# Gate products of a recurrent block: fp32 matmuls, or three products of high and low halves split on GpSimd

## What is computed

```
gate_br, x_br = split(h @ w_in, 2)                      # w_in: 1024 x 2560
gate_br = gelu(gate_br)
xc = conv_b + sum(xp[:, j:j+S] * conv_w[j] for j in range(4))      # causal, 1280 channels
r = sigmoid(einsum('bsnd,nde->bsne', xc, ga_w) + ga_b)  # 10 blocks of 128 x 128
i = sigmoid(einsum('bsnd,nde->bsne', xc, gx_w) + gx_b)  # 10 blocks of 128 x 128
log_a = -8 * r * softplus(-lam)
a, mult = exp(log_a), sqrt(-expm1(2 * log_a))
h_t = a_t * h_(t-1) + mult_t * (i * xc)_t               # scan over the tokens
out = (h * gate_br) @ w_out
```

## Time and profile before

| | |
|---|---|
| time, median of 3 runs | 1376.95 us (1376.85 to 1377.02) |
| profiled execution, its own time | 1376.97 us |
| its span in the profile | 1375.1 us |
| TensorE busy | 1361.9 us (99%) |
| VectorE busy | 1119.8 us (81%) |
| ScalarE busy | 930.9 us (68%) |
| GpSimd busy | 89.2 us (6%) |
| DMA | 319 GB/s in the mean |
| granted TensorE clock | 0.998 |
| recurrent block, projections and gates | 315 to 376 us of the span |

### The profile page before, as it was taken

The page is one execution under the profiler, slowest core; times in us unless marked ns, Lnnn a source line. Parts: engine busy times, 40 slices in busy tenths (PEclk is TensorE's granted clock), DMA queues, the critical chain, the costliest instruction groups (busy, mean ns, idle before and its releaser), DMA issues.

```text
span 1375.1 us, 18249 instructions
## 1 busy us (share of the span) xinstructions
PE 1361.9 (99%) x6778; PEld 1152.6 (84%) x6778; DVE 1119.8 (81%) x952; ACT 930.9 (68%) x734; POOL 89.2 (6%) x89
## 2 busy tenths in 40 slices
PE   9999999999999999999999999999999999999997
PEld 9988888889988888888888888888888888888885
DVE  6776554458979999898888989889898898989896
ACT  5756444445858777777777777777777677777764
POOL 4000000001220000000000000000000000001130
PEclk9999999999999999999999999999999999999999
DMA  9535655652569999999999999999999999999993
GB/s 309 188 132 174 214 186 189 236 178 93 184 236 368 411 401 366 395 407 345 391 393 361 370 394 411 336 398 390 360 377 386 411 340 397 389 356 381 409 367 120
DMA packets 147266, 438.33 MB, mean 319 GB/s; under 512 B 7267, under 2 KB 30428, under 8 KB 147218
## 3 DMA queue, kind: packets, MB, share of 16 engines
q1 hardware_dynamic: 142848, 423.39, 81.6%
q0 software_dynamic: 4304, 14.27, 3.4%
q10 hardware_dynamic: 66, 0.02, 0.0%
HBM read 429.35 MB, written 8.40 MB: 318 GB/s over the span
## 4 chain that ended last, share of the span: by engine, by line
PE 97%; DMA 1%; ACT 1%; DVE 1%; issue 0%; POOLq 0%; SPq 0%; DVEq 0%; ACTq 0%
PE ps L1936 29%; PE ps L1525 27%; PE ps L1941 14%; PE ps L1953 14%; PE ps L1958 7%; PE ps L1977 2%; DMA work<-in_moe_w_down_dram 1%; PE ps L1816 1%; PE ps L2037 0%; PE ps L1611 0%; PE ps L1741 0%; DMA xres<-in_x_dram 0%; PE ps L1874 0%; ACT w_hi L532 0%; PE ps L1581 0%
## 5 line engine op out<-in xcount | busy, mean ns | idle before, releaser
L532 ACT ACTIVATE w_hi<-w_ring 128x2048 fp32r<-128x2048 f32 (+1 forms) x258 | 487.6, 1902 | 162.2 <-PE ps L1941 90.3
L1395 DVE TENSOR_TENSOR w_lo<-w_ring,w_hi 128x2048 fp32r<-128x2048 f32 x190 | 433.7, 2301 | 56.2 <-ACT w_hi L532 55.8
L532 ACT ACTIVATE w_hi<-work 128x2048 fp32r<-128x2048 f32 x144 | 275.3, 1918 | 122.7 <-PE ps L1958 63.7
L1395 DVE TENSOR_TENSOR w_lo<-work,w_hi 128x2048 fp32r<-128x2048 f32 x141 | 322.7, 2302 | 39.7 <-ACT w_hi L532 39.2
L1936 PE MATMUL ps<-w_hi,xt_hi 128*128 128x512 f32 x896 | 289.5, 393 | 0.8 <-ACT xt_hi L532 0.8
L1936 PE MATMUL ps<-w_hi,xt_lo 128*128 128x512 f32 x896 | 286.8, 390 | 0.0
L1941 PE MATMUL ps<-w_lo,xt_hi 128*128 128x512 f32 x896 | 239.7, 389 | 0.0
L1953 PE MATMUL ps<-w_hi,split 128*128 128x512 f32 x864 | 214.4, 390 | 0.2 <-DVE split L1405 0.2
L1936 PEld LDWEIGHTS ps<-w_hi,xt_lo 128*128 128x128 f32 x896 | 168.2, 188 | 35.4
L1941 PEld LDWEIGHTS ps<-w_lo,xt_hi 128*128 128x128 f32 x896 | 168.2, 188 | 35.3
L1936 PEld LDWEIGHTS ps<-w_hi,xt_hi 128*128 128x128 f32 x896 | 165.8, 188 | 33.9 <-issue 1.0
(11 more groups left out here) (293 smaller groups left out, 1177.6 us busy)
## 6 DMA issues: line engine op xcount, KB each, us to landing
w_ring<-in_moe_w_up_dram SPq DMA_DIRECT2D x72, 1024.0 KB, 8.8
w_ring<-in_moe_w_down_dram SPq DMA_DIRECT2D x72, 1024.0 KB, 6.8
work<-in_moe_w_gate_dram SPq DMA_DIRECT2D x64, 1024.0 KB, 8.2
w_ring<-in_moe_w_gate_dram SPq DMA_DIRECT2D x48, 1024.0 KB, 7.9
work<-in_moe_w_up_dram SPq DMA_DIRECT2D x40, 1024.0 KB, 8.7
work<-in_moe_w_down_dram SPq DMA_DIRECT2D x40, 1024.0 KB, 6.7
w_ring<-in_attn_w_qkv_dram SPq DMA_DIRECT2D x11, 1024.0 KB, 11.2
w_ring<-in_ffn_w_gate_dram SPq DMA_DIRECT2D x11, 1024.0 KB, 5.1
```

What stands on the lines that cost most here:

```text
L532: return nc.scalar.activation(out, in_, ACT.Copy)
L1395: V.tensor_tensor(w_lo[:, half_slot(n), :], land(n), w_hi[:, half_slot(n), :].bitcast(F32), ALU.subtract).then_inc(lo_ready, 1)
```

## The change

The gates take the form of the other products. The gate weights and the convolved inputs are split into a high half (fp32r) and the rest, both on GpSimd. The halves lie in parts of `split` that are free at that time; `wga_lo` takes columns of `aT_hi` and so waits for `piece_used`, `P_IN`. `split_xc(j)` has one buffer and waits for the gates of the pair before (`ri_ps`). PE waits for `wg_lo` instead of `in_lru` ahead of the second piece, and for `xc_lo_ok` instead of `xc_ok` ahead of the gates.

```diff
+        wga_lo = split[:, 0:1280].rearrange("p (n e) -> p n e", n=RB)
+        xc_hi = split[:, 1280:1792].rearrange("p (n t) -> p n t", n=2)
+        xc_lo = split[:, 1792:2304].rearrange("p (n t) -> p n t", n=2)
+        wga_hi = split[:, 2304:3584].rearrange("p (n e) -> p n e", n=RB)
+        wgx_hi = split[:, 3584:4864].rearrange("p (n e) -> p n e", n=RB)
+        wgx_lo = split[:, 4864:6144].rearrange("p (n e) -> p n e", n=RB)
...
+            pool.wait_ge(in_lru, 32)
+            for hi, w in ((wga_hi, wga), (wgx_hi, wgx)):
+                nc.gpsimd.tensor_copy(hi, w).then_inc(wg_hi, 1)
+            pool.wait_ge(wg_hi, 2)
+            nc.gpsimd.tensor_tensor(wgx_lo, wgx, wgx_hi.bitcast(F32), ALU.subtract).then_inc(wg_lo, 1)
+            pool.wait_ge(piece_used, P_IN)
+            nc.gpsimd.tensor_tensor(wga_lo, wga, wga_hi.bitcast(F32), ALU.subtract).then_inc(wg_lo, 1)
+
+            def split_xc(j):
+                pool.wait_ge(xc_ok, j + 1)
+                if j:
+                    pool.wait_ge(ri_ps, j)
+                nc.gpsimd.tensor_copy(xc_hi, xc[:, j % 2]).then_inc(xc_hi_ok, 1)
+                pool.wait_ge(xc_hi_ok, j + 1)
+                nc.gpsimd.tensor_tensor(xc_lo, xc[:, j % 2], xc_hi.bitcast(F32), ALU.subtract).then_inc(xc_lo_ok, 1)
+
             for j in range(RB // 2):
+                split_xc(j)
                 pool.wait_ge(ri_ok, 2 * j + 2)
...
-            pe.wait_ge(in_lru, 32)
+            pe.wait_ge(wg_lo, 2)
 
             def gates(j):
-                pe.wait_ge(xc_ok, j + 1)
+                pe.wait_ge(xc_lo_ok, j + 1)
                 if j:
                     pe.wait_ge(t_ok, 2 * j)
                 for m in range(2):
-                    for w, bank in ((wga, 2), (wgx, 3)):
-                        ins = T.matmul(ps[:, bank, 256 * m:256 * m + 256], w[:, 2 * j + m, :], xc[:, j % 2, m, :],
-                                       start=True, stop=True)
+                    b = 2 * j + m
+                    for wh, wl, bank in ((wga_hi, wga_lo, 2), (wgx_hi, wgx_lo, 3)):
+                        ins = mm3(ps[:, bank, 256 * m:256 * m + 256], xc_hi[:, m, :], xc_lo[:, m, :], wh[:, b, :], wl[:, b, :],
+                                  True, True, True)
```

More of the change, by code:

```diff
@@ L351, in build_trunk @@
         sroot_ps, sroot_ok = sem("sroot_ps"), sem("sroot_ok")
+        wg_hi, wg_lo, xc_hi_ok, xc_lo_ok = sem("wg_hi"), sem("wg_lo"), sem("xc_hi_ok"), sem("xc_lo_ok")
         root_ps, gate_raw, ixs_ok = sem("root_ps"), sem("gate_raw"), sem("ixs_ok")
```

## The result

The changed kernel took **1390.01 us** (median of 6, 1388.80 to 1391.32) against 1376.95: ratio 1.0095, 95% interval [1.0085, 1.0105]. That is 13 us slower; 1381.9 was forecast, with 1388.5 as the upper end. The direction was right, the size was not. The six times lie in two groups, three at 1388.8 and three at 1391.2 to 1391.3. The profiled execution is of the second: 1391.22 us, span 1389.4, clock 0.993.

What follows compares the result with a forecast made beforehand. TensorE was taken to bound the kernel, with VectorE close behind. Gate stalls of 2.75 + 1.0 + 0.8 + 1.0 + 0.8 = 6.35 us, less 1.45 gained, added 4.9 to 1376.97: 1381.9 us, range 1376.5 to 1388.5.

Steps and rivals of the forecast that it cites:

- Twelve products: TensorE's gates: 1.44 us a pair instead of 1.73 for four fp32 products, 1.45 us gained over five pairs.
- The conversion: GpSimd's high half of xc: taken as 0.6 us, with bounds of 0.6 and 2.4 us.
- the subtraction: GpSimd's low half of xc: priced at 1.15 to 1.2 us of work by the same engine's tensor_tensor.
- The weights' split: GpSimd's split of the gate weights: ends by 312.8, PE asks at 315, so it costs nothing.
- its race against w_lo in pair 0: First gates: w_lo runs until 322.48, then the subtraction; PE starts at 323.8 instead of 321.05, a 2.75 us stall.
- The conversion hides beside w_lo in this sum if it isn't excluded too: Pair 0's split on GpSimd: the 0.6 us conversion runs during VectorE's w_lo and adds nothing to the 2.75 us stall.
- I go by the row: Choice against B: a w_lo starting inside a one-input GpSimd tensor_scalar took its usual 2.28 us; own forecast 45%.
- rival B: Conversion of xc excluded beside w_lo too: stalls sum to 10.5 us, less 1.45, giving 1386.0 us; chance 28%.
- odd pairs: Gates of pairs 1 and 3: the split arrives behind ix, stalling PE 1.0 us each; B had 0.7.
- the range's margin: The only place where a clock fall after TensorE's waits was counted; range 1376.5 to 1388.5 us.
- no row shows it fall after a wait of 3 us: TensorE's clock: taken as full over this stretch; a fall would come on top of B or C.
- C: Conversion of xc costs its upper bound, 2.4 us: stalls sum to 15.0 us, less 1.45, giving 1390.5 us; chance 10%.

Runs made afterwards that it cites:

- spread3: spread2 with the first half of the third piece's w_lo moved behind the next four xt_lo; 1375.55 us, ratio 0.9990.
- spread2: Changed kernel with the pairs' work moved from GpSimd to ScalarE and VectorE, w_lo halved, third w_lo and table load earlier, first gates inside next piece; 1376.63 us.
- act_cast: Changed kernel with the conversion of xc on ScalarE instead of GpSimd, the subtraction staying on GpSimd; 1381.68 us.
- warm: Changed kernel with dummy products on TensorE into an unused PSUM bank ahead of each gate wait; 1386.20 us.
- again: Changed kernel executed once more for its profile, with only a blank line added in the source; 1388.83 us.
- split_first: Changed kernel, but VectorE starts the w_lo behind each xc only when GpSimd has split that xc; 1387.21 us.
- pool_alone: Changed kernel with all of GpSimd's new work, but TensorE keeping its four fp32 gate products and waiting for xc as before; 1380.12 us.
- after: The changed kernel itself, in its profiled execution, of the slower group of times; 1391.22 us.
- idle: Kernel before, fp32 gates and nothing split, with TensorE held ahead of gates 0, 2 and 4 by GpSimd memsets of unused columns; 1387.10 us.
- pe_alone: Changed kernel with twelve products a pair but no split of xc on GpSimd, its low part left out; weights still split; 1376.41 us.

## Why the prediction was wrong, point by point

**Right.** Twelve products cost 1.44 us, and 5 x 0.29 is the gain wherever TensorE sets the round (spread3). The conversion costs 0.60 us, by the copies of the earlier trace rows; the subtraction 1.26. The weights' split is free: it ended at 311.5, and PE didn't wait at 315 (spread2 shows what it costs when a w_lo half stands beside it). That the subtraction loses its race against w_lo in pair 0: act_cast, which leaves just that, had its first gates at 323.68 for my 323.8. act_cast's time of 1381.7 does not prove the rest of the sum, since its later pairs went by another chain.

**The step that failed** is "The conversion hides beside w_lo in this sum if it isn't excluded too", and the choice behind it, "I go by the row". It is excluded. The first stall was 3.22 us for my 2.75 and rival B's 3.45, the second 2.16 for my 0.8 and B's 1.75, and the last 4.1 for my 0.8 and B's 3.9, since the conversion came between the first and the second of the three w_lo, the subtraction between the second and the third. The waits were 9.5 us for my 6.35. warm's time is B's sum to 0.2 us, but in part by balance: against rounds of 7.19 us its five gates came 3.3, 1.2, 1.4, 1.2 and 3.4 us later, where B had 3.45, 0.7, 1.75, 0.7 and 3.9. B was wrong on the odd pairs, in which `ix` went ahead of w_lo. The Trainium skill, page "SBUF — State Buffer", section "Who interferes with whom", has a VectorE instruction with two SBUF inputs contend with a GpSimd instruction that reads SBUF; the runs agree (2.61 against 0.60 us, and 0.61 in all five pairs once w_lo stood behind). I had set against it one row, a GpSimd tensor_scalar beside an undisturbed w_lo. What I had not looked at is that row's beginning. In the trace of before, the w_lo ahead of it:

```profile
1303.68 3.90 DVE L1395 TENSOR_TENSOR w_lo<-work,w_hi 128x2048 fp32r<-128x2048 f32 x1 [1.85 <-ACT w_hi L532]
```

It had itself started beside a GpSimd tensor_tensor that ran from 1303.02 to 1305.43, and it ran until 1307.6, over the first 2.0 of the tensor_scalar's 4.78 us. The row so contains a stretch in which it may have been the one held, and may have been done with its reads when the next w_lo began at 1308.64. This was only argued, no run took it apart; but a row with such a neighbour could not carry the choice, and did not bound the conversion at 2.4 us either.

**The term that was missing** is the lower clock: 6.2 us of slow products in the profiled execution, 2.6 to 5.0 us in the time by warm, left in "the range's margin". The profiled execution lost 9.4 us more than my 4.9: 3.1 are the waits (9.5 for 6.35), 6.2 the clock. The sentence "no row shows it fall after a wait of 3 us" was true because the trace has no wait of 3 us, so it was no evidence. On top of B's 1386.0, 2.6 to 5.0 us give 1388.6 to 1391.0; that this is where both groups are is no second proof, since the cost was taken from these times. The range's upper end, 1388.5, was B with 2.5 us of margin: a cost that would come on top of B and could not be excluded should have been priced as one.

**A term that was mis-sized by luck**: odd pairs. I had 1.0 and B 0.7 for each; they had 0 in the profiled execution, and in again one of them 0.9. With TensorE at the lower level its round was stretched from 7.2 to 9.9 us, so that GpSimd had caught up: `ix`, conversion and subtraction of pair 1 were done at 332.95, and PE came at 334.2. Part of the price of the clock was paid with the stalls of the odd pairs (in warm, at full clock, they are back), so the two can't simply be added.

**A rival that came near by chance**: C, a conversion of 2.4 us everywhere, had 1390.5 us, and 1390.0 was measured. Its condition failed: with no w_lo in the way the conversion took 0.60 to 0.61 us (pairs 1 and 3 of the changed kernel, all five pairs of split_first).

**Overlooked**: VectorE has work with one SBUF tensor that GpSimd holds, the tensor_scalars. GpSimd's new work cost 3.2 us in pool_alone, where my sum had nothing for it. In the changed kernel it is hidden behind the stalls (VectorE stands for 4.56 and 3.60 us behind the two stretched rounds); it shows once these are gone.

## What to carry over

A chain of two short operations on GpSimd, handed over between VectorE instructions that read two SBUF tensors, costs the length of those instructions and not its own: 1.9 us of work arrived 4.0 us after `xc`. Before GpSimd is given work beside a VectorE that is busy for most of its round, price each of its instructions as if it started after the running VectorE one, and each following VectorE one as if it waited for it; then ask where TensorE will stand still, for behind the waits of 3.2 us here the lower clock took another 1.8 to 2.7. And a gain on the engine that bounds (0.29 of 7.48 us here) is only to be had when the next engine's round is shorter than the new one: here that took moving work between three engines, for 0.1%.

## What the hardware showed that I had not expected

- A VectorE tensor_scalar of 128x256 with one SBUF tensor was held by GpSimd: two took 1.64 to 1.66 us instead of 0.74 beside a subtraction (after, warm) and 2.65 beside a subtraction and `ix` (pool_alone). The six taps (two SBUF tensors each) took 3.6 to 3.8 instead of 2.7 beside `ix`. The Trainium skill, page "VectorE: DVE Perf Modes", section "Mode 2×_2P — use both read ports for one tensor", names tensor_scalar as an operation that can use both ports for its one tensor. The stretched rows fit that; which mode the instruction ran in, no row shows.
- After 3.2 to 3.5 us without work TensorE ran at the lower level, 1.2 GHz, in each of the three runs shown (after, again, idle): at once or from within its first microsecond of work on, and for 3 to 6 us. After 2.05 to 2.16 us it did so in some places and not in others, in the same kernel. The changed kernel's time has two values, 2.4 us apart.
- GpSimd's prices with no VectorE instruction in the way: conversion of 128x512 to fp32r 0.60 to 0.61 us, of 128x1280 1.23 (pe_alone); subtraction of 128x512 1.26; memset of 128x3840 3.30 us (idle).
